# Feed-forward of a hybrid layer: gate and up by Strassen block products, the middle tiles through DRAM, the embedding product in front

## The reference, cut to what matters

```python
hf = rmsnorm(x, norm_ffn_g)
x = x + (jax.nn.silu(hf @ w_gate) * (hf @ w_up)) @ w_down      # 1024 -> 2816 -> 1024
g = jax.nn.sigmoid(rmsnorm(x, norm_ple_g) @ w_ple_gate)        # 1024 -> 1024
x = x + g * (p @ w_ple)                                        # 256 -> 1024
y = rmsnorm(x, final_norm_g)
```

## Time and profile before

| what | value |
|---|---|
| device time, median of 3 runs | 2689.96 us (2687.56 to 2692.24) |
| span of the profiled execution | 2689.6 us |
| feed-forward and end, from the end of `stage_out` to the end | 1699.3 to 2689.6 us of the span |
| TensorE busy | 2613.3 us, 97% |
| VectorE, ScalarE busy | 56%, 33% |

### The profile page before, as it was taken

How to read it: one execution, slowest core, us unless ns; L and a number is a source line. 1 busy time by engine, 2 the same in 40 slices (tenths; PEclk the granted TensorE clock), 3 DMA queues, 4 the chain that set the end, 5 groups by cost and what they waited for, 6 DMA issues and landing times. The chain is left out here.

```text
span 2689.6 us, 47862 instructions
## 1 busy us (share of the span) xinstructions
PE 2613.3 (97%) x17088; PEld 2490.4 (93%) x17088; DVE 1493.0 (56%) x2513; ACT 876.8 (33%) x1708; POOL 345.1 (13%) x327
## 2 busy tenths in 40 slices
PE   6999999999999999999979999999999999999897
PEld 6888888888879999999979999999999999999897
DVE  4666766766675666666643443545444444444754
ACT  4433444434342636363631122211111111111513
POOL 0222322322231111111100002000000000000300
PEclk8999999999999999999979999999999999999999
DMA  7544544435645242424155433411111111111112
GB/s 135 90 107 81 100 100 93 101 79 108 75 75 67 30 103 32 100 33 101 32 202 186 162 102 125 145 40 47 39 39 47 39 45 40 39 47 39 36 41 81
DMA packets 331843, 214.21 MB, mean 80 GB/s; under 512 B 117828, under 2 KB 312216, under 8 KB 331672
## 3 DMA queue, kind: packets, MB, share of 16 engines
q1 hardware_dynamic: 331672, 211.98, 34.3%
HBM read 164.51 MB, written 47.41 MB: 79 GB/s over the span
## 5 line engine op out<-in xcount | busy, mean ns | idle before, releaser
L165 PE MATMUL bank<-operand_hi,w_hi 128*128 128x384 f32 x1584 | 532.9, 336 | 1.5 <-DVE w_lo L148 1.5
L165 PE MATMUL bank<-operand_hi,w_lo 128*128 128x384 f32 x1584 | 530.0, 335 | 0.0
L165 PE MATMUL bank<-operand_lo,w_hi 128*128 128x384 f32 x1584 | 529.9, 335 | 0.0
L139 ACT ACTIVATE w_hi<-w_raw 128x1024 fp32r<-128x1024 f32 (+1 forms) x167 | 172.7, 1034 | 782.0 <-PE bank L165 486.9
L165 PEld LDWEIGHTS bank<-operand_hi,w_hi 128*128 128x128 f32 x1584 | 297.5, 188 | 2.1 <-issue 1.8
L165 PEld LDWEIGHTS bank<-operand_lo,w_hi 128*128 128x128 f32 x1584 | 297.5, 188 | 0.3
L165 PEld LDWEIGHTS bank<-operand_hi,w_lo 128*128 128x128 f32 x1584 | 297.4, 188 | 0.0
L694 PE MATMUL acc<-operand_hi,w_hi 128*128 128x384 f32 x792 | 281.9, 356 | 6.4 <-PEq L215 6.4
L1153 POOL TENSOR_TENSOR wgt<-wgt,left 128x128 f32<-128x128 f32 (+2 forms) x224 | 210.1, 944 | 588.2 <-DVE left L1105 423.1
L694 PE MATMUL acc<-operand_hi,w_lo 128*128 128x384 f32 x792 | 267.8, 338 | 0.0
L694 PE MATMUL acc<-operand_lo,w_hi 128*128 128x384 f32 x792 | 267.2, 337 | 0.0
(11 more groups left out here) (356 smaller groups left out, 4457.8 us busy)
## 6 DMA issues: line engine op xcount, KB each, us to landing
w_raw<-in_w_in SPq DMA_DIRECT2D x65, 512.0 KB, 8.7
k_cache<-in_cache_k SPq DMA_DIRECT2D x256, 64.0 KB, 2.5
v_cache<-in_cache_v SPq DMA_DIRECT2D x64, 256.0 KB, 4.4
w_raw<-in_w_gate SPq DMA_DIRECT2D x22, 512.0 KB, 3.9
w_raw<-in_w_up SPq DMA_DIRECT2D x22, 512.0 KB, 3.8
w_raw<-in_w_down SPq DMA_DIRECT2D x22, 512.0 KB, 3.6
s_gate_a<-gate SPq DMA_DIRECT2D x24, 192.0 KB, 2.8
s_o<-o_t SPq DMA_DIRECT2D x8, 576.0 KB, 10.8
```

Source lines behind the costliest of these rows:

```text
L139: act.activation(hi, S.raw[u0 % 2][:, 0:cols], ACT.Copy).then_inc(S.hi_done, 1)
L165: last = pe.matmul(acc[:, 0:RBN], w[:, k, :], a[:, k, rows], start=(n == 0), stop=(n == 3 * kts - 1 and more is None))
```

## The change

The feed-forward becomes two phases with a pass through DRAM between them, and the embedding product moves ahead of both.

- `stage_out` no longer makes the high and low part of the operand. It writes the plain product of x and gain (`S.xg`). In its last pass TensorE also transposes p (`turn_p`), and ScalarE and VectorE split it.
- `stage_up` begins with the whole embedding product (24 blocks of 6 matmuls), which ScalarE copies out of PSUM (`read_emb`) and SyncE stores to DRAM (`s_embedding`). Meanwhile the row factors are made and the operand is prepared: the four quarters of the operand (half of the inputs by half of the rows) are scaled by VectorE and GpSimd, combined into `t1` to `t4`, and seven of them split into high and low.
- Then 22 steps, one for each feed-forward tile. The weights' four quarters (gate and up, by halves of the inputs) are combined by GpSimd into four `comb` tiles. Seven products of 4 input tiles by 3 matmuls by 2 halves of 288 rows (24 matmuls of 128x288 each) take the place of 144 matmuls of 128x384. VectorE and ScalarE put the results together (U2, T1, U3, C22, C21, H1, C12, T2, H2), 576 columns at a time, and SyncE stores the two halves of the hidden tile (`s_hidden`).
- `stage_down` reads the hidden tiles back in pairs and makes 11 passes of 24 blocks as before, now without gate and up in between. x comes from DRAM at its beginning.
- `stage_end` makes only the gate products and loads the embedding tiles from DRAM.

The core of the diff (the new functions cut to what sets the order):

```diff
+def stage_up(nc, S, A, b0, u0):
...
+    def sync(sp):
+        def load(m, par):
+            for w, dst in zip((A.w_gate[0], A.w_up[0]), raws[par]):
+                sp.dma_start(dst[:, :].rearrange("p (k c) -> p k c", k=KT), wsrc(w, m * P)).then_inc(raw_in[par], 16)
...
+        for i, par in steps(sp.Fori):
+            if not isinstance(i, int):
+                sp.wait_ge(wl_done, done(i, NP - 1) - NP)
+                load(i + 1, 1 - par)
+            sp.wait_ge(ev, element(i, E_H1))
+            store(i, 0, c21[par], h1_st[par])
+            sp.wait_ge(ev, element(i, E_H2))
+            store(i, 1, c22[par], h2_st[par])
...
+        for n in range(24):
+            ple(n)
+            if n == 2:
+                sums_of_rows()
+            if n == 6:
+                spread()
+
+        def product(i, par, n):
+            pe.wait_ge(wl_done, done(i, n))
+            if isinstance(i, int) and i == 0:
+                pe.wait_ge(a_lo, (1, 3, 3, 4, 5, 6, 7)[n])
...
+            elif fresh[n]:
+                pe.wait_ge(ev, element(i, (E_T1, E_U2, None, E_C21, E_C12)[n] - NE))
+            if n == 2:
+                pe.wait_ge(kept_done, START + i + 1)
+            if n == 5:
+                pe.wait_ge(ev, element(i, E_U3))
+            if n == 6:
+                pe.wait_ge(ev, element(i, E_C22))
...
+            for s in range(2):
+                cols = slice(s * UN, (s + 1) * UN)
+                for k in range(KH):
+                    for m, (w, a) in enumerate(((hi, a_h), (hi, a_l), (lo, a_h))):
+                        first = fresh[n] and k == 0 and m == 0
+                        last = pe.matmul(q[:, s, :], w[:, k, :], a[:, k, cols], start=first,
+                                         stop=(k == KH - 1 and m == 2), skip_group_check=not fresh[n])
...
+        for i, par in steps(act.Fori):
+            if isinstance(i, int) and i == 0:
+                continue
+            more = not (isinstance(i, int) and i == LASTP)
+            keep(i)
+            if more:
+                w_hi(i + 1, 1 - par, 0)
+                w_hi(i + 1, 1 - par, 1)
+            sigmoid_one(i)
+            if more:
+                for n in range(2, 6):
+                    w_hi(i + 1, 1 - par, n)
+            sigmoid_two(i)
+            if more:
+                w_hi(i + 1, 1 - par, 6)
...
+            if more:
+                w_lo(i + 1, 1 - par, 1)
+            t1_(i)
+            if more:
+                w_lo(i + 1, 1 - par, 2)
+            u3(i, par)
...
+        dve.nop().then_inc(S.lo_done, 2)
...
+            if n == 0:
+                wait_raw(pool, m, par)
...
+            a, b, op = ((w21, w22, ALU.add), (comb[0][:, :], w11, ALU.subtract), (w11, w21, ALU.subtract),
+                        (w12, comb[1][:, :], ALU.subtract))[n]
+            pool.tensor_tensor(comb[n][:, :], a, b, op).then_inc(comb_done, 1)
...
+def stage_down(nc, S, A, b0, bv0, u0):
...
+        S.W.load(sp, u0, 2, 0, down_tile(A, 0, 0))
+        S.W.load(sp, u0 + 1, 2, 0, down_tile(A, 0, 1))
+        for s in U.h_st:
+            sp.wait_ge(s, DMA_HEAD + 16)
+        load_hid(0, 0)
+        sp.wait_ge(U.pr_done, START + NP * U.LASTP + 2)
         for k in range(KT):
             sp.dma_start(x[:, k, :], S.d_x[k]).then_inc(x_in, 16)
...
+        S.W.split_lo(dve, u0, 2, 0, None)
+        lows(0, 0, 0)
+        lows(0, 0, 1)
+        S.W.split_lo(dve, u0 + 1, 2, 0, None)
+        dve.wait_ge(x_in, 16 * KT)
```

More of the change, by code:

```diff
@@ L2077, in block, with turn_p @@
                           more=add_x, before=before)
+        def turn_p(m):
+            pe.wait_ge(p_in, 32)
+            if m >= 2:
+                pe.wait_ge(plo_done, m - 1)
+            for r in range(3):
+                last = pe.transpose(sums[m % 2][:, r * P:(r + 1) * P],
+                                    p_rows[:, 3 * (m // 2) + r, (m % 2) * P:(m % 2 + 1) * P], S.ident[:, :])
+            last.then_inc(pt_done, 1)
         pe.wait_ge(S.merged, 3 * (KT - 2))
@@ L2085, in tensor, with body @@
             block(0, n, merged_in)
-        with pe.Fori(1, KT // 2) as i:
+        with pe.Fori(1, LAST) as i:
             for n in range(6):
                 block(i, n)
+        for n in range(6):
+            block(LAST, n)
+            turn_p(n)
     def scalar(act):
-        for s in (hi_done, sq_done):
+        for s in (xg_done, sq_done):
             act.nop().then_inc(s, START)
-        with act.Fori(0, KT // 2) as i:
+        def body(i, last):
             for n in range(6):
@@ L2147, in down_tile @@
         .rearrange("a p k c -> (a p) k c")
-def stage_ffn(nc, S, A, ctx, own, b0, bv0, u0, next_tiles):
-    N = FT // 2
[L2154 to L2175, removed]
-    S.f = Store()
[L2177 to L2197, removed]
-    def sync(sp):
[L2201 to L2205, removed]
@@ L2218, in tensor @@
[L2218 to L2228, removed]
+        sp.wait_ge(U.pr_done, START + NP * FT)
@@ new lines, in sync @@
+        sp.wait_ge(U.ev, START + NE * FT)
+        for s in U.h_st:
+            sp.wait_ge(s, DMA_HEAD + 16 * N)
+        for i, par in passes(sp.Fori):
+            if isinstance(i, int):
+                for j in range(2):
+                    S.W.load(sp, u0 + 2 + j, 2, i, gate_tile(A, j))
+                break
+            sp.wait_ge(al_done, 2 * i + 2)
+            load_hid(i + 1, 1 - par)
+            for j in range(2):
+                S.W.load(sp, u0 + 2 + j, 2, i, down_tile(A, i + 1, j))
@@ L2469, in vector @@
-        steps.end(1)
-        with dve.Fori(1, N) as i:
-            steps.body(i - 1, F_PASS)
-            gate_up(i, "up0", 0)
-            down(i)
-            lows(i, 0)
-            gate_up(i, "up1", 1)
-            lows(i, 1)
-            steps.end(0)
-        down(N, final=True)
+        S.W.split_lo(dve, u0, 2, 0, None)
[3 more added lines that the diff above has]
+        dve.wait_ge(x_in, 16 * KT)
+        for i, par in passes(dve.Fori):
+            down(i, par, isinstance(i, int))
@@ L2515, in stage_end @@
-    gates, embs, sums = S.bank[3:6], S.bank[0:3], S.bank[6:8]
+    gain, junk, out0, out1 = [at(n, [P, D], F32, 8 * T + 4 * D * m)[:, :] for m, n in enumerate(("gain", "junk", "out0", "out1"))]
+    emb_t = [at(f"emb{n}", [P, ROWS], F32, f.hid1 + T * n) for n in range(2)]
+    out = [out0, out1, S.ss[:, 0:D]]
+    gates, sums = (S.bank[3:6], S.bank[0:3]), S.bank[6:8]
     yt = S.pair[1:4]
     mean_sq, last_sq, part_var, var, root, rfac = [
-        sb(n, [P, RT]) for n in ("mean_sq", "last_sq", "part_var", "row_var", "row_root", "row_rstd")]
@@ L2553, in first_emb_block @@
-    def first_emb_block(pe, rb):
-        if rb == 0:
-            pe.wait_ge(plo_done, 6)
-            pe.wait_ge(S.lo_done, HEAD + u0 + 2)
-        pe.wait_ge(S.acc_read_v, HEAD + bv0 - 2 + rb)
-        product(pe, embs[rb], *f.first_emb, (p_hi, p_lo), rb, 2)
-    def sync(sp):
-        sp.wait_ge(S.acc_done, HEAD + b0)
-        sp.dma_start(gain, A.final_norm_g.unsqueeze(0).to_broadcast([P, D])).then_inc(gain_in, 16)
-        with sp.Fori(0, N - 2) as i:
-            for j in range(2):
-                S.W.load(sp, u0 + 4 + j, 2, i, ple_tile(A, i + 2, j))
+                pe.wait_ge(S.lo_done, HEAD + uw + 1)
@@ L2867, in hybrid_step @@
         u, b = u + 8 * NG, b + 8 * NRB * NG
-        with ExitStack() as banks, ExitStack() as late:
+        with ExitStack() as banks:
             with ExitStack() as end:
```

934 lines of the change are left out of this document (600 added, 334 removed).

## The result

The changed kernel takes 2698.6 us (median of 15 runs, 2694.5 to 2703.5), the kernel before, run beside it, 2691.3 us (15 runs). The ratio is 1.0023, 95% interval 1.0015 to 1.0031: 6 us slower by the ratio, 7 by the medians, where 35 us faster was forecast and 2688 was the upper end of the range. The profiled span is 2698.9 us. `stage_out` ends at about 1694.6 us in both traces, so all of the difference lies behind it. (The kernel before starts its first block of gate and up at 1694.5 us; the 1699.3 us given for the end of `stage_out` ahead of the prediction is 4.8 us late, so the stretch is 995 us long and holds some 46 us beside its matmuls, not 41. No term of the sum hangs on it.)

What follows compares the result with a forecast made beforehand. TensorE, busy 97% of the span, bounds the kernel. Terms -68.8 + 12.4 + 3.2 + 4.0 + 5.4 + 12.8 - 5.5 + 1.3 = -35.2 us on 2689.6 give 2654.4, stated as 2655; 8-in-10 range 2636 to 2688.

Steps and rivals of the forecast that it cites:

- signs of being wrong: Stated as showing the forecast wrong: 288-column starts much over 134 ns apart, or a step over 24.3 us.
- The loop of the step: Steps of phase one: chain of 22.5 us against TensorE's 21.84, a loss of 12.4 us over steps 2 to 20.
- rival 2: Loop: chain longer but still pays; combinations 1.6 us, landing 7 us, step 23.2 to 24.1, 2668 to 2685; chance 0.15.
- The front: Before and under the embedding product: net +4.0 us ahead of it, then +5.4 for late products 0, 1, 5 and 6.
- 2.1 for the clock: After the idle stretch before the first embedding block: a restart at low clock costs TensorE 2.1 us.
- the layout of VectorE's nine passes at 2.55 us and GpSimd's three at 5.3: Operand preparation under the embedding product's 25 us of TensorE, laid out by list; products late by +5.4 us.
- The products: Gate and up: 3696 matmuls of 288 columns at 0.130 us replace 3168 of 384; 549.3 to 480.5 us, gain 68.8.
- my bracket: Time of a 288-column matmul: 0.126 to 0.1334 us around 0.130; gain 83.6 or 56.3 us at the ends.
- Rival 4: Gate and up: a matmul costs its weight load, 173.4 ns at 288 columns, step 29.1 us, total 2800; chance 0.05.
- Between the phases: From last H2 to first down product: TensorE starts at 16.7 us; net +12.8 with clock and old wait counted.
- The end: Gate blocks and tail: gate waits mostly go, -5.5 us; last embedding block and later table loads, +1.3.
- Rival 3: Loop: the chain eats the gain; pair of loads lands at 9.7 us, step 26.0, 2721 us, slower; chance 0.10.

Runs made afterwards that it cites:

- Runs 1 to 4: The first of them issues 12 matmuls more in each step of the changed kernel: 2699.4 us, ratio 1.0035; the others are run 2, run 3 and run 4.
- run 5: Changed kernel with the front's operand arithmetic on VectorE alone and ScalarE copying the last embedding blocks before splitting operands: 2696.4 us, ratio 1.0023.
- run 2: Changed kernel with SyncE issuing the weight loads one step ahead, before it waits for the step's two stores: 2665.5 us, ratio 0.9903.
- run 6: Changed kernel with the second phase's first loads and splits moved into the last step of phase one: 2683.3 us, ratio 0.9965.
- run 8: Changed kernel with loads a step ahead, early second phase, and front arithmetic on VectorE alone with T2 in its own buffer: 2646.2 us, ratio 0.9822.
- run 3: Changed kernel with sigmoid, T1 and U3 ahead of the next step's weight splits, loads still late: 2668.5 us, ratio 0.9914.
- run 4: Changed kernel with GpSimd doing the first combination of each step's weights once more, ahead of the real one: 2745.8 us, ratio 1.0193.

## Why the prediction was wrong

The kernel's shape was read rightly: TensorE gains, a chain binds the steps at U3, the gap between the phases is 16.7 us. The sizes of the loop and of the two parts of the front were not, all in one direction, and the gain of 35 us was smaller than their sum. Neither of the prediction's own signs of being wrong came (288 columns over 134 ns apart, a step over 24.3 us): they watched for one large miss, and several smaller ones came together. Span against sum: 2698.9 - 2654.4 = 44.5 us.

**The loop of the step, the term that failed most.** I had 22.5 us and 12.4 us for the steps 2 to 20; from 1788.98 to 2244.25 us they took 455.3, where 19 x 22.5 is 427.5: 27.8 of the 44.5 us. The links of one step (2029.55 to 2053.32), measured and predicted: products 5 and 6 with the handover to C12 6.7 (6.25); C12 to H2 3.1 (3.4); H2 to the second landing 6.6 (6.2); two combinations 3.2 (2.65); from there to product 5 4.2 (4.0). Landings I had nearly right. By these durations more than half of the 1.3 us is GpSimd and VectorE beside each other: the second combination took 1.63 us for 1.27, the low parts 1.10 for 0.69; no run takes GpSimd out of the loop, so this share is read from the trace and not tested. I named that resource, allowed 0.4 us a step for it at most and put the 1.6 us only into rival 2, whose step of 23.2 to 24.1 us is what came (23.83). The other piece is that steps 2 and 3 took 24.8 and 25.3 us, step 3 with 3.4 us at the low clock (1815.1 to 1818.5). The prediction also said that nearly all of VectorE's operations in a step read two SBUF inputs; 10 of the 16 do, and those that read a PSUM bank keep their 0.74 us where GpSimd works beside them. Runs 1 to 4 show the chain from four sides: work for TensorE is free, an earlier load or a shorter queue behind it frees 29 to 32 us, a longer link costs more than its length.

**The front.** From the first embedding block to product 0 I had 25.0 us of blocks, 2.9 for 27 small matmuls (which the prediction held level with the old form's), 2.1 late and 2.1 for the clock, 32.1; it took 39.95, +7.9 (seven traces with this front have 38.2 to 41.3). From product 0 to the wait of step 1: 43.9 (a step of 21.84, 3.3 of waits, five products, 3.2), measured 49.7, +5.8. The step that failed is the layout of VectorE's nine passes at 2.55 us and GpSimd's three at 5.3. Side by side five of VectorE's passes took 2.56 or some 7.5 us, by who had started first, and GpSimd's three 7.5 (run 5). The Trainium skill (GPSIMD Engine Reference, "Key points") has GpSimd contending with VectorE operations that read two SBUF inputs, and this trace agrees: at 2304 columns VectorE's take up to three times their 2.5 us. In sum the pair gains nothing, since the times add up: three passes of VectorE and two of GpSimd took 17.5 us (1712.8 to 1730.3), where five of VectorE alone, at run 5's rate, are 12.5. Embedding copies stood behind the splits on ScalarE (3.6 and 4.6 us of TensorE), and products 0 and 1 then ran at 240 ns a matmul for 3.6 to 4.1 us each. Run 5 shows that mending this alone gives nothing that can be measured at the end.

**The products.** 288 columns start 132.8 ns apart, at the 133.4 end of my bracket and not at 130: 3696 x 0.1328 is 490.8 us, a gain of 58.5 in place of 68.8. In the changed kernel this costs little beyond the links of products 5 and 6, since the chain is longer than 22.3 us anyway; in run 2 it is the bound. Rival 4, that a matmul costs its weight load (640.9 us), is refuted by that distance.

**Between the phases** the estimate was right: 16.70 us measured, 16.7 predicted, and run 6 gets 16 of them back, so the gap was an order of queues and not a price of the change. **The end:** steps 20 and 21 behind the wait took 0.6 us more than nine products at 3.12; what is left of the 44.5 is 2.4 us, behind the start of the second phase. From the last gate matmul to the end the trace has 18.5 us where the kernel before had 16.9 and the prediction added 0.3, which is 1.3 of it; no run tests why.

**The rivals.** Rival 3 (slower, by a landing of 9.7 us) gave the right sign for a wrong reason: the loads landed 4.1 and 5.3 us after their issue. The new time came from rival 2's step and a front that no rival had. I treated chain, front and clock as separate small risks, where one cause, two engines on one resource, lengthened both of the first two: shown for the front by run 5, read from durations alone for the loop.

**What the change is worth.** With its three waits mended the same arithmetic takes 2646 us, 1.8% less than the kernel before (run 8): the 58 us of TensorE's work less some 11 that the front and the rest keep.

## What to carry to other kernels

When a change shortens the work of the busiest engine in a loop, add up the longest chain that closes on itself through the other queues, and price its links as they run beside each other, not alone; a margin of 3% between chain and engine is no margin. Then ask of each queue in the chain what stands ahead of the releasing operation only by the order of the list: moving three operations (run 3) or the loads (run 2) was worth all of the loss here and 23 to 26 us more. A second engine that reads the same memory may bring nothing: time both together before work is split between them, and look at single operations, since the mean of a short and a long one can hide that they take turns.

## What the runs showed of the hardware that was not expected

- VectorE and GpSimd side by side, 2304 columns, two inputs from SBUF: VectorE 2.56 us when it started first and 7.4 to 7.6 when not, alone 2.5; GpSimd 7.5. At 512 columns, in the loop: GpSimd 1.3 us when it started first, 1.6 to 1.8 when not; VectorE 1.1 to 1.3 when GpSimd had started first, 0.68 while GpSimd was idle. VectorE's operations that read a PSUM bank stayed at 0.74 us beside it.
- A wait of 1.1 to 1.4 us in each step left the granted clock at 1.00 (changed kernel, 1836 to 2214 us); a wait of 2.6 us brought it to the low level, 240 ns a matmul for some 3.3 us, after 10 of that stretch's 15 waits (run 4). A wait can thus cost more than itself, and inside a closed chain the slow stretch lengthens the next step too.
- 288 float32r columns start 132.8 ns apart, 12.8 over the 120 of 288 columns at 2.4 GHz; 384 columns have 13.4 over theirs.
